# Channel mixers of a decoder trunk: weight blocks as the stationary operand in chunks 3 to 9

## The reference, cut to what matters

```python
D_MODEL = 1024; SEQ = 256; D_FF = ((8 * D_MODEL // 3 + 255) // 256) * 256   # 2816

def swiglu(x, w_in, w_out):
    gate, up = jnp.split(x @ w_in, 2, axis=-1)
    return (jax.nn.silu(gate) * up) @ w_out

x = layer_norm(ALPHA * x + 0.5 * swiglu(x, ffn1_w_in[l], ffn1_w_out[l]), ...)
# ... the layer's token mixer and its norm ...
x = layer_norm(ALPHA * x + 0.5 * swiglu(x, ffn2_w_in[l], ffn2_w_out[l]), ...)
```

## Time and profile before

| | |
|---|---|
| median of three runs | 967.49 us |
| the profiled execution: span from its first to its last instruction | 966.1 us |
| outside the span, by the difference to the median | 1.4 us |
| TensorE busy with matmuls | 956.1 us (99%) |
| VectorE (DVE) busy | 848.8 us (88%) |
| ScalarE (ACT) busy | 564.8 us (58%) |
| GpSimd (POOL) busy | 37.9 us (4%) |
| DMA engines, mean busy share of the main queue | 54.5% |

### The profile page before, as it was taken

One profiled execution on the slowest core, in us unless ns is written; L12 is line 12 of the kernel. 1 busy time (PEld: TensorE's weight loads), 2 busy tenths in 40 slices (PEclk: granted clock), 3 DMA queues, 4 the chain that ended last, 5 costly groups with the idle time before them and its releaser, 6 DMA issues.

```text
span 966.1 us, 12770 instructions
## 1 busy us (share of the span) xinstructions
PE 956.1 (99%) x4520; PEld 792.9 (82%) x4520; DVE 848.8 (88%) x1208; ACT 564.8 (58%) x627; POOL 37.9 (4%) x64
## 2 busy tenths in 40 slices
PE   9999999999999999999999999999999999999996
PEld 7888888888888888888888888888888888888885
DVE  5999888996888999899899998999898998888896
ACT  6665556436645555565565555549898545565650
POOL 0100000000210000000000000000100100000000
PEclk9999999999999999999999999999999999999999
DMA  9686566553657565665566565735233655565631
GB/s 305 221 267 239 195 199 222 190 181 125 225 196 237 179 213 179 213 217 174 177 216 216 174 218 179 257 113 192 88 132 121 228 196 193 180 215 176 214 133 43
DMA packets 129312, 184.47 MB, mean 191 GB/s; under 512 B 5968, under 2 KB 104800, under 8 KB 129136
## 3 DMA queue, kind: packets, MB, share of 16 engines
q1 hardware_dynamic: 126032, 173.56, 54.5%
q0 software_dynamic: 2672, 9.77, 2.8%
q10 hardware_dynamic: 560, 0.52, 0.2%
HBM read 182.78 MB, written 1.05 MB: 190 GB/s over the span
## 4 chain that ended last, share of the span: by engine, by line
PE 95%; DVE 3%; ACT 1%; issue 0%; DMA 0%; POOL 0%; DVEq 0%; ACTq 0%
PE psum L1711 29%; PE psum L1720 29%; PE psum L1715 29%; PE psum L1886 2%; PE psum L2235 1%; PE psum L1704 1%; PE psum L2221 1%; DVE w_lo L937 0%; DMA raw<-in_ffn_w_in 0%; ACT w_hi L482 0%; PE psum L1970 0%; PE psum L1990 0%; PE psum L2207 0%; DVE w_lo L967 0%; PE psum L2039 0%
## 5 line engine op out<-in xcount | busy, mean ns | idle before, releaser
L937 DVE TENSOR_TENSOR w_lo<-raw,w_hi 128x2048 fp32r<-128x2048 f32 x125 | 284.8, 2282 | 7.5 <-ACT w_hi L482 7.3
L1711 PE MATMUL psum<-w_hi,xT 128*128 128x512 f32 x959 | 266.1, 394 | 0.6 <-DVE arena L1469 0.4
L1720 PE MATMUL psum<-w_hi,xT 128*128 128x512 f32 x959 | 261.7, 390 | 0.2 <-DVE xT L1011 0.2
L1715 PE MATMUL psum<-w_lo,xT 128*128 128x512 f32 x959 | 261.5, 389 | 0.0
L482 ACT CAST w_hi<-raw 128x2048 fp32r<-128x2048 f32 x125 | 238.7, 1916 | 23.0 <-DMA raw<-in_ffn_w_in 16.1
L1720 PEld LDWEIGHTS psum<-w_hi,xT 128*128 128x128 f32 x959 | 180.1, 188 | 38.5 <-DVE xT L1011 0.5
L1715 PEld LDWEIGHTS psum<-w_lo,xT 128*128 128x128 f32 x959 | 180.0, 188 | 37.6
L1711 PEld LDWEIGHTS psum<-w_hi,xT 128*128 128x128 f32 x959 | 176.8, 188 | 37.4 <-DVE ffn_tok L1069 1.3
L519 ACT ACTIVATE ffn_tok<-psum 128x256 f32<-128x256 f32 x88 | 33.8, 384 | 204.3 <-PE psum L1715 195.4
L1711 PE MATMUL psum<-w_hi,hT_hi 128*128 128x512 f32 x316 | 99.5, 403 | 0.0
L1715 PE MATMUL psum<-w_lo,hT_hi 128*128 128x512 f32 x316 | 95.6, 391 | 0.0
(11 more groups left out here) (202 smaller groups left out, 817.9 us busy)
## 6 DMA issues: line engine op xcount, KB each, us to landing
raw<-in_ffn_w_in SPq DMA_DIRECT2D x170, 512.0 KB, 4.8
raw<-in_ffn_w_out SPq DMA_DIRECT2D x88, 512.0 KB, 4.0
raw<-in_c_w_in SPq DMA_DIRECT2D x32, 512.0 KB, 4.5
raw<-in_ab_w_in SPq DMA_DIRECT2D x16, 512.0 KB, 4.8
raw<-in_ab_w_o SPq DMA_DIRECT2D x8, 512.0 KB, 3.7
raw<-in_c_w_o SPq DMA_DIRECT2D x8, 512.0 KB, 3.7
ln_gb<-in_ln_gain POOLq DMA_DIRECT2D x6, 512.0 KB, 6.4
ln_gb<-in_ln_bias POOLq DMA_DIRECT2D x6, 512.0 KB, 7.2
```

The source lines that it names most:

```text
L937: nc.vector.tensor_tensor(w_lo[:, slot_of[n]], raw[:, n % RAW], w_hi[:, slot_of[n]].bitcast(F32), ALU.subtract).then_inc(lo_ready, 1)
L1711: nc.tensor.matmul(dst, a_hi, b_hi, start=first, stop=False)
L1715: ins = nc.tensor.matmul(dst, a_hi, b_lo, start=False, stop=final and last)
L1720: ins = nc.tensor.matmul(dst, a_lo, b_hi, start=False, stop=final and last)
```

## The change

In chunks 3 to 9 of each channel mixer (seven chunks, four mixers, 28 chunks) the roles are exchanged. The weight block (128 input features x 128 hidden features) is stationary, and x moves, its high part and its rest side by side as 512 columns. A chunk has four such blocks of hidden features: gate and up of the first 128 (b = 0, 1), gate and up of the second 128 (b = 2, 3). Each block is 8 matmuls of 512 columns with the high weights and 8 of 256 columns with the rest of the weights. The bank then holds two halves, high-x and rest-x, that still have to be added. ACT copies the whole bank to SBUF (`up_copy`). For blocks 0, 1 and 2 a DMA issued by POOL adds the second half to the first (`add_halves`, `accum_op=ALU.add`); for block 3 DVE adds them (`last_up_add`). ACT takes the silu in SBUF (`up_silu`), DVE multiplies (`up_product`). The result already has the hidden features on the partitions, so these chunks have no transposes.

All four blocks use the same bank `G[0]`, and each waits until ACT has copied the one before. The down matmuls are spread between the blocks: 6, 5, 5 and 5 of them. Two of the seven products (3 and 6, "late") run another chunk later. The hidden values are cast in two pieces (640 and 256 columns) instead of one of 896. The loop on TensorE is written out. The work of `layer_c_tables` moves from chunk 3 to chunk 2, and POOL issues the adds of chunks 3 and 4 of the first mixer ahead of four table loads.

```diff
-            def loop_chunk(name, s0, i, par, c, last=False):
...
-                pe.wait_ge(hidT_copied, c + N_COPY * f)
-                project(n, i, 0, G[0])
-                products(name, n + 2, i, c - 1, (0, 1, 2), plain_used, False, last)
-                pe.wait_ge(hid_ready, c * 2 + (hid + 1))
-                project(n, i, 1, G[0])
-                products(name, n + 2, i, c - 1, (4, 6), pairs_done if last else None, False, last)
+            def up_block(name, n, c, b):
+
+                before = 4 * (N_FM * SILUS[name] + c - FIRST_FM) + b
+                j, g = divmod(b, 2)
+                if c == FIRST_FM and b == 0:
+                    pe.wait_ge(hidT_copied, N_COPY * (SILUS[name] + 1))
+                else:
+                    pe.wait_ge(up_copied, before)
+                for kh in range(2):
+                    pe.wait_ge(hi_ready, nth[n + kh])
+                    for k in range(4):
+                        at = k * 512 + g * FC + j * P
+                        nc.tensor.matmul(G[0], w_hi[:, slot_of[n + kh], at:at + P],
+                                         xT_both[:, 4 * kh + k].rearrange("p a s -> p (a s)"),
+                                         start=kh == k == 0, stop=False)
+                for kh in range(2):
+                    pe.wait_ge(lo_ready, nth[n + kh])
+                    for k in range(4):
+                        at = k * 512 + g * FC + j * P
+                        ins = nc.tensor.matmul(G[0][:, 0:SEQ], w_lo[:, slot_of[n + kh], at:at + P],
+                                               xT_hi[:, 4 * kh + k], start=False, stop=kh == 1 and k == 3)
+                ins.then_inc(up_done, 1)
...
+                for c in range(FIRST_FM, NC - 1):
+                    feature_chunk(name, s0, c)
+                late_products(name, s0 + FFN_UNITS - 5, NC - 3, True)
```

ACT's list, with the copy and the silu:

```diff
+            def up_copy(name, c, b):
...
+                act.wait_ge(up_done, 4 * (N_FM * f + c - FIRST_FM) + b + 1)
+                if c > FIRST_FM:
+                    act.wait_ge(hid_product, 2 * (N_FM * f + c - FIRST_FM - 1) + b // 2 + 1)
+                dst = HALVES[name][b]
+                nc.scalar.copy(dst, G[0]).then_inc(up_copied, 1)
+
+            def up_silu(name, c, j):
+
+                act.wait_ge(halves_added[2 * j], 16 * (N_FM * SILUS[name] + c - FIRST_FM + 1))
+                gate = HALVES[name][2 * j][:, 0:SEQ]
+                nc.scalar.activation(gate, gate, ACT.Silu).then_inc(gate_silu, 1)
```

DVE's list for chunks 4 to 9 (chunk 3 has `hidden_sums` first), and POOL's adds:

```diff
+                        last_up_add(name, c - 1)
+                        weight_sums(name, n, 0)
+                        up_product(name, c - 1, 1)
+                        hidden_sums(name, c - 1)
+                        weight_sums(name, n, 1)
+                        split_lo(n + 1)
+                        hid_early_lo(name, c - 1)
+                        hid_late_lo(name, c - 1)
                     beside(name, c)
...
+                    split_lo(n + 2)
                     split_sums_lo(name, n)
+                    up_product(name, c, 0)
...
+            def add_halves(name, chunks=range(FIRST_FM, NC - 1)):
+                for c in chunks:
+                    for b in range(3):
+                        block = 4 * (N_FM * SILUS[name] + c - FIRST_FM) + b + 1
+                        pool.wait_ge(up_copied, block)
+                        both = HALVES[name][b]
+                        pool.dma_start(both[:, 0:SEQ], both[:, SEQ:], accum_op=ALU.add).then_inc(halves_added[b], 16)
```

More of the change, by code:

```diff
@@ L36 @@
 N_PROD = NC - 2
-N_COPY = NC - 1
+N_COPY = 3
+FIRST_FM = 3
+N_FM = NC - 1 - FIRST_FM
+STD_CHUNK = {0: 0, 1: 1, 2: 2, NC - 1: 3}
+N_T = N_COPY + 2
 N_STD = 2 * NC + 2
@@ L1680, in _ @@
                     load_gb(n)
+                if name in FFN:
+                    add_halves(name, range(5 if name == "F0" else FIRST_FM, NC - 1))
                 norm(n)
@@ new lines, in product, with high, weight_rest @@
+            def product(p, a, w, stop=False):
+                slot, part = B_OF[p]
+                return nc.tensor.matmul(PROD[p], a[:, A_OF[p] * P:(A_OF[p] + 1) * P],
+                                        w[:, slot, part * 512:(part + 1) * 512], start=False, stop=stop)
+            def high(*which):
+                for p in which:
+                    ins = product(p, hT_hi_flat, w_hi)
+                return ins
+            def weight_rest(*which):
+                for p in which:
+                    ins = product(p, hT_hi_flat, w_lo)
+                return ins
@@ new lines, in token_rest, with token_chunk @@
+            def token_rest(last, *which):
+                for p in which:
+                    ins = product(p, hT_lo_flat, w_hi, last and p in ALONE)
+                return ins
+            def token_chunk(name, s0, c):
+                f, n = SILUS[name], s0 + 3 * c - 1
+                p, hid, hidden = n + 2, 2 * f * len(STD_CHUNK) + 2 * c, NH * f + c
+                pe.wait_ge(hidT_copied, N_COPY * f + c)
+                project(n, None, 0, G[0])
+                pe.wait_ge(hidT_hi, hidden)
+                pe.wait_ge(plain_hi, nth[p])
+                high(0, 1, 2)
+                pe.wait_ge(plain_lo, nth[p])
+                weight_rest(0, 1, 2)
+                pe.wait_ge(hid_ready, hid + 1)
+                project(n, None, 1, G[0])
+                pe.wait_ge(hidT_lo, hidden)
+                token_rest(False, 0, 1, 2).then_inc(plain_used, 1)
+                pe.wait_ge(sums_hi, nth[p])
+                high(4, 5)
+                pe.wait_ge(sums_lo, nth[p])
+                weight_rest(4)
+                hidden_T(name, ((c * 2, ffn_tok[:, 1, 0]), (c * 2 + 1, ffn_tok[:, 1, 1])), G[0])
+                weight_rest(5)
+                token_rest(False, 4, 5).then_inc(early_used, 1)
+                pe.wait_ge(late_hi, N_PROD * f + c)
+                high(3, 6)
```

290 lines of the change are left out of this document (205 added, 85 removed).

## The result

The changed kernel takes 1000.63 us as the median of four runs (998.39 to 1003.51), against 967.39 us for the kernel before on the same chip: a ratio of 1.034, interval 1.033 to 1.035. The prediction said 962.2 us. The kernel is 33 us slower than before, which is the first rival's case and lies outside the range.

What follows compares the result with a forecast made beforehand. TensorE, busy 99% of the span with no long waits, was taken as the bound. Span 966.1 - 7.8 + 1.5 + 1.0 = 960.8 us, with the median 1.4 above it, gave 962.2 us; range 958 to 974.

Steps and rivals of the forecast that it cites:

- the first rival: Block 2's add reaches the second silu late, 28 x (latency - 5.0); at 5.5 us 14 us, 976 us; chance 0.25.
- The adding DMAs: POOL's three adds a chunk: landing taken as 4.4 us between 1.9 and 6.4, cost nothing; at 6.4, 39 us.
- the limit of 5.0 us: Block 2's add, issued at 8.7, may take 3.7 us with no effect and 5.0 before TensorE stands.
- the text's own price: Late adds of block 2 at the second silu cost 28 x (latency - 5.0).
- the limit that the text gives for it: Block 1's add, issued at 4.8, is wanted by DVE's product at 8.8, with 1.3 more before DVE's room is used up.
- the range's end at 974: Upper end of the range that leaves out two in ten, for an add of 5.4 us.
- the text's own bound: Upper end taken for an adding DMA's landing, 6.4 us, costing 1.4 us in each of 28 chunks.
- The change on TensorE: In 28 chunks, exchanged matmul shapes cost +0.168 us, dropped transposes save 0.447: -0.279 us a chunk, -7.8 us in all.
- the model of 16.09: Old chunk on TensorE as 69 x 0.2267 + 0.447 = 16.09 us, a check on the 16.12 us read.
- The bank and ACT: ACT's copy between blocks fits behind five down matmuls with about 0.07 us to spare, ACT being free: cost nothing.
- The lag of 1.5 us: In F2's chunks 3 to 6 DVE's 16.4 us exceeds the new chunk length: +1.5 us, bounds 0 and 2.3.
- the term of 1.0 us: In chunk 2 ACT's copy of the transposed values delays TensorE's first block: +0.25 us four times, bounds 0 and 2.

Runs made afterwards that it cites:

- Run 4: The changed kernel with the weight loads of chunks 2 to 9 bringing only a quarter of their bytes, adds unchanged: 978.27 us (one run).
- run 7: The changed kernel with plain copies of the same bytes on POOL's queue in place of the adding DMAs: 981.86 us (one run).
- run 1: The changed kernel without the adding DMAs and the waits on them: 970.23 us, ratio 1.0025 to the kernel before.
- Run 2: The changed kernel with the three adding DMAs of a chunk replaced by additions on DVE: 974.65 us, 1.007 to the kernel before.
- Run 9: The kernel with all adds on DVE, with nine down matmuls again before chunk 2's second projection and layer C's tables beside chunk 3: 974.29 us.
- run 6: The changed kernel with DVE subtracting only 512 of 2048 columns of two weight units in chunks 3 to 9: 1000.49 us (one run).
- run 10: The changed kernel with second silu and products later, mixer heads as before, DMA adds only in F2's chunks 3 to 8, DVE adds elsewhere: 971.13 us.
- run 8: The kernel with second silu and products moved later, with DVE also making the adds of each mixer's chunk 9: 975.91 us.
- run 11: The kernel without adds, plus 84 copies of 2 KB on POOL's queue that no other engine waits for: 974.98 us.
- runs 3: The changed kernel with ACT's second silu behind the next weight cast and DVE's products behind weight work, adding DMAs kept: 978.6 us, 1.0109 to the kernel before.
- run 5: The changed kernel with the three adds of a chunk computed by POOL itself instead of adding DMAs: 983.46 us, 1.0155 to the kernel before.

## Why the prediction was wrong

**The step that failed** is the sized term in "The adding DMAs": "Ends: 1.9 and 6.4; I take 4.4, the middle of the three near rows. Cost at 4.4: nothing." The adds of block 2 took 6.1 us. The place, the chain and the limit of 5.0 us were right. By the text's own price that is 28 x (6.1 - 5.0) = 31 us. Measured by the medians it is 1000.63 - 970.23 - 2.5 (the program's end) = 27.9 us. That the two come so close is partly luck. The loss isn't 28 equal pieces: chunk 4 of F0 and F3 takes 15.71 us with the adds and without, the steady chunks of F0, F1 and F3 lose 0.7 to 1.6 us each, F2's chunk 3 loses 3.1 (with the low clock), and three tails, which the prediction hadn't looked at, take 10.4 us instead of 8.7.

What was wrong was to take the middle of three single rows for a transfer that had to stay below 5.0 us 28 times. It wasn't the company of weight loads that these rows lacked. In the kernel before, the DMA engines were as busy while these transfers ran (64 KB, 128 KB, 256 KB) as they were beside block 2's adds in F3's chunks 4 and 5 (columns as above, the DMA share is the last but one):

```profile
24.08:29.08 5.00, 5.00 (x26) 4.13 (x25) 4.71 (x9) 3.62 (x4) 4.37 (x7) 1.00 0.82 251
26.11:29.77 3.66, 3.66 (x18) 3.03 (x17) 3.41 (x6) 2.93 (x3) 2.34 (x5) 1.00 0.87 259
65.51:70.00 4.49, 4.49 (x23) 3.75 (x22) 4.19 (x8) 3.08 (x4) 2.35 (x4) 1.00 0.84 276
```
```profile
878.50:884.84 6.34, 6.34 (x36) 5.46 (x35) 3.67 (x5) 2.07 (x2) 0.84 (x1) 1.00 0.95 276
895.53:902.30 6.77, 6.77 (x40) 5.88 (x38) 4.08 (x6) 2.07 (x2) 0.85 (x1) 1.00 0.85 240
```

The DMA share counts these transfers too. By the DMA records the hardware loads alone took 62 to 68% of the engines' time in the three stretches, and 69% in the median beside the 28 adds of block 2.

Run 4 shows that the lateness needs the loads, with landings of 2.7 and 3.3 us once they are light. But beside loads a landing scatters, from 2.7 to 7.4 us in the changed kernel, and three rows of 3.7 to 5.0 don't show that. The second part is the addition, which the sum put at nothing: in block 2 a plain copy landed after 5.1 us in the median and the add after 6.1 (run 7). These 1.0 us are more than half of the miss of 1.7. How much of the rest comes from standing behind block 1's add in the same queue, no run takes apart. Block 1's add, too, broke the limit that the text gives for it (8.8 + 1.3 - 4.8 = 5.3 us, measured 6.5), and DVE waited 39.6 us for it. In the stretch shown above it is block 2's chain that holds TensorE up, but no run removes block 1's add alone. With a slope of 28 us per us beyond a threshold that stands 0.6 us above the value taken, a chance of 0.25 looks too low, and the range's end at 974 had stopped at 5.4 us although the text's own bound was 6.4.

**The change on TensorE**: forecast -0.279 us a chunk and -7.8 in all, measured -0.19 and -5.3. The 256-column distance is 0.120 instead of 0.1186 (0.04 us a chunk), and 21 down matmuls in four short groups take 4.87 us instead of 4.76. The chunk's own 16.12 had contained 0.03 that the model of 16.09 didn't.

**The bank and ACT**: right. Without adds the copy fits each time (run 1), with 3.93 us from block to block on TensorE.

**DVE**: right that it is full in F2's chunks 3 to 6 and has room elsewhere. Run 2 turns this into numbers: there three more additions per chunk cost 4 us in F2 and nothing in most steady chunks of the others. The lag of 1.5 us was well sized: in run 1, F2's chunks 3 to 6 take 16.56, 15.96, 16.19 and 16.19 us, 1.2 us over four times 15.93.

**Chunk 2**: the wait that the term of 1.0 us priced does occur, but it costs 0.2 us, and a larger one beside it was missed. Run 1's weight loads (total us, times, longest), and TensorE at the two places in F0:

```profile
PEld psum L1828 <- DVE ffn_tok L1158: 3.9, 4, 1.5
...
PEld psum L2020 <- ACT arena L546: 1.1, 4, 0.5
```
```profile
41.92 0.84 PE L2034 MATMUL psum<-w_lo,hT_hi 128*128 128x512 f32 x3
...
43.58 1.20 PE L1828 MATMUL psum<-w_hi,xT 128*128 128x512 f32 x4 [0.82 <-DVE ffn_tok L1158]
...
51.65 0.62 PE L2034 MATMUL psum<-w_hi,hT_hi 128*128 128x512 f32 x2
...
52.31 1.68 PEld L2020 LDWEIGHTS psum<-xT,w_hi 128*128 128x128 f32 x8 [0.47 <-ACT arena L546]
```

L546 is the copy of the transposed values, the wait that I read. Block 0 starts at 52.31, where 51.65 + 2 x 0.227 = 52.10 was due, and in the other mixers nothing is lost. L1158 is DVE's product ahead of the second projection, which now has six down matmuls in front of it instead of nine. That projection starts at 43.58, where 41.92 + 3 x 0.227 = 42.60 was due, and the same wait costs 1.20 us in F1 and 0.59 in F2, 2.8 us together. The diff showed it, but I hadn't counted it. Run 9 puts the nine matmuls back and regains only 0.4 us, so the missing cover alone isn't the cause: DVE is late there.

**Where the gain went**: heads, tails and F2 cost 6.9 us over the floor of the chunks where 2.5 were forecast. In run 1 these waits are 2.8 us of it, three tails of 8.7 us instead of 8.4 are 0.9, and DVE's lag in F2 is 1.2. The rest is spread in pieces that no run took apart.

**What the prediction had not asked about**: the program's end, 2.5 us of the 33, and that of the adds in each mixer's last exchanged chunk, where no next chunk hides them.

**Alone and in company.** The five adds that I followed, which met no load at their start, had their last packet 2.3 to 2.8 us after the issue and the shortest landing was 2.7, so the 2.3 us by the Trainium skill ("DMA: Bandwidth & Descriptors", "Anatomy of one DMA — SWDGE (gpsimd) path") come near for an add alone and fail beside loads, 5.8 in the median. The same page of the Trainium skill ("Queues, rings and completion order") says that an engine takes turns between its queues packet by packet. By that an add's first packet would wait for one packet of a load, and here it comes up to 3.2 us later than alone, some of that behind the add before it in the same queue. Whether it is held up in that turn or earlier, when its descriptors are made, stays open: run 4 takes away the loads and doesn't tell these apart. The warning of the Trainium skill ("SBUF — State Buffer", "SBUF: two separate sides"), that DVE may hold up POOL's descriptors, finds no sign here: run 6 cut two of DVE's weight splits per chunk to a quarter and left the landings as they were (5.3 and 6.0 us).

## What to carry to other kernels

Ask of a new DMA in a loop not how long it takes but how long it may take, and count how few rows it rests on: three transfers of one queue don't show how its landings scatter beside loads, and none of them was an addition. If the limit lies inside the bounds and the loop runs 28 times, the slope decides, not the middle value. When a profile names a copy or a cast as the releaser, read that engine's list backwards until an instruction is found that itself waited. And work taken off a steady loop has to be counted against what it does to the first and last chunks: here a gain of 5.3 us in the loop was used up by heads, tails and a full DVE in one mixer.

## What the hardware showed unexpectedly

- **The last drain of POOL's queue.** 2.11 us in the kernels where POOL issues 25 DMAs in the program, 3.58 with 43 of which 18 add (run 10), 6.64 with 97 of which 72 add (run 8), 8.56 with 109 where 84 are copies, of 2 KB or of 128 KB (runs 7 and 11), and 5.17 with 109 where 84 are additions (the changed kernel and runs 3, 4, 6). It was longer in every kernel that issued more than 25, but it doesn't follow the count alone, and by what rule it goes is open.
- **An adding DMA of POOL beside hardware loads**: its first packet starts 1.4 us after its issue when no load is under way, and in the median 3.7 us after it in the changed kernel. Even a copy of 2 KB lands after 1.6 us at the least, 3.0 in the median and 6.2 at the most (run 11).
- **POOL's own additions slow DVE**: a subtraction of 2048 columns by 12% and one of 256 by 64%, in the mean of the groups that run beside them (run 5).
- **TensorE's clock behind one wait**: in the profiled execution of the changed kernel the granted clock fell to 1.2 GHz for 3.4 us right behind a wait of 1.86 us, and in run 5's, at 520 us, behind one of 1.94.
